# Keys turned later, vector work dealt out anew and a new layout of activations in a two-block transformer kernel

## What is computed

```
h  = modulate(rms_norm(x), shift, scale);  hc = the same for ctx
q, k, v = split(h @ w_qkv); q = rms_norm(q) * q_g; k = rms_norm(k) * k_g   # per head; k, v also of hc
s  = [q k^T / sqrt(128) + bias, masked;  q kc^T / sqrt(128)];  o = softmax(s) [v; vc]
x  = x + gate_msa * (o @ w_o)
x  = x + gate_ffn * (silu(conv3(h2 @ w_gate)) * conv3(h2 @ w_up)) @ w_down
```

## Time and profile before

| | |
|---|---|
| median of 3 runs | 2519.28 us (2518.7 to 2519.54) |
| the profiled execution | 2518.32 us, span 2516.6 us |
| PE busy | 2468.2 us, 98% of the span, 13260 matmuls |
| DVE, ACT, POOL busy | 71%, 46%, 9% |
| chain that ended last | PE 88%, DVE 5%, DMA 4%, issue 2%, ACT 1% |
| DMA | 519.06 MB, mean 206 GB/s |

### The profile page before, as it was taken

How to read it: one execution, slowest core, us unless ns; L and a number is a source line. 1 busy time by engine, 2 the same in 40 slices (tenths; PEclk the granted TensorE clock), 3 DMA queues, 4 the chain that set the end, 5 groups by cost and what they waited for, 6 DMA issues and landing times.

```text
span 2516.6 us, 38054 instructions
## 1 busy us (share of the span) xinstructions
PE 2468.2 (98%) x13260; PEld 2119.8 (84%) x13260; DVE 1786.5 (71%) x2395; ACT 1161.1 (46%) x1512; POOL 218.1 (9%) x251
## 2 busy tenths in 40 slices
PE   9999999999999999998999999989999999999999
PEld 8989988888888888887887888877888888888887
DVE  6667757898888877876666776776667656665666
ACT  4455545534535445553223333334555535553453
POOL 5000000000000000312111011130200000000000
PEclk9999999999999999999999999999999999999999
DMA  8655577887787778756556565665655665656665
GB/s 268 183 135 154 165 252 243 278 292 238 262 274 240 263 241 277 242 166 182 171 178 191 186 186 180 197 202 156 191 188 183 194 194 175 193 191 194 182 187 173
DMA packets 281385, 519.06 MB, mean 206 GB/s; under 512 B 33822, under 2 KB 105256, under 8 KB 280512
## 3 DMA queue, kind: packets, MB, share of 16 engines
q1 hardware_dynamic: 255968, 403.67, 51.0%
q0 software_dynamic: 25120, 113.89, 14.4%
q10 hardware_dynamic: 192, 0.05, 0.0%
HBM read 515.35 MB, written 6.90 MB: 208 GB/s over the span
## 4 chain that ended last, share of the span: by engine, by line
PE 88%; DVE 5%; DMA 4%; issue 2%; ACT 1%; POOL 0%; DVEq 0%; SPq 0%; POOLq 0%; ACTq 0%
PE ps L2029 33%; PE ps L2058 22%; PE ps L2061 11%; PE ps L2435 11%; PE ps L2021 3%; DMA arena<-in_w_ada 2%; DVE arena L1572 2%; PE ps L2513 1%; PE ps L2494 1%; DVE wlo L1240 1%; PE ps L2446 1%; DMA raw<-in_na_w_qkv 1%; DMA raw<-in_w_in 1%; PE ps L2503 1%; PE ps L2350 0%
## 5 line engine op out<-in xcount | busy, mean ns | idle before, releaser
L1240 DVE TENSOR_TENSOR wlo<-raw,whi 128x1024 fp32r<-128x1024 f32 (+1 forms) x776 | 930.4, 1210 | 411.8 <-ACT whi L727 390.2
L727 ACT ACTIVATE whi<-raw 128x1024 fp32r<-128x1024 f32 (+1 forms) x776 | 797.0, 1036 | 840.4 <-PE ps L2029 372.2
L2029 PE MATMUL ps<-whi,act 128*128 128x512 f32 (+3 forms) x2736 | 823.8, 382 | 11.3 <-POOL act L694 5.7
L2058 PE MATMUL ps<-act,whi 128*128 128x512 f32 x2400 | 657.6, 395 | 1.4 <-DVE act L1903 1.3
L2029 PEld LDWEIGHTS ps<-whi,act 128*128 128x128 f32 x2736 | 505.0, 188 | 104.5 <-POOL act L694 5.7
L2029 PE MATMUL ps<-wlo,act 128*128 128x512 f32 (+3 forms) x1368 | 520.0, 380 | 0.0
L2058 PEld LDWEIGHTS ps<-act,whi 128*128 128x128 f32 x2400 | 410.1, 189 | 56.6 <-DVE act L1903 1.6
L2061 PEld LDWEIGHTS ps<-act,wlo 128*128 128x128 f32 x2400 | 369.5, 189 | 51.7
L2061 PE MATMUL ps<-act,wlo 128*128 128x256 f32 x2400 | 383.9, 281 | 0.0
L2435 PE MATMUL ps<-whi,act 128*128 128x512 f32 x1024 | 325.0, 399 | 1.6 <-issue 1.6
L1572 DVE SCALAR_TENSOR_TENSOR arena<-arena,cond 128x768 f32<-128x768 f32 (+1 forms) x330 | 291.2, 905 | 19.4 <-DMA arena<-in_w_ada 16.0
(11 more groups left out here) (317 smaller groups left out, 1776.9 us busy)
## 6 DMA issues: line engine op xcount, KB each, us to landing
arena<-in_w_ada POOLq DMA_DIRECT2D x128, 768.0 KB, 6.1
raw<-in_ffn_w_up SPq DMA_DIRECT2D x160, 512.0 KB, 4.3
raw<-in_w_mlp_in SPq DMA_DIRECT2D x128, 512.0 KB, 4.8
raw<-in_w_mlp_out SPq DMA_DIRECT2D x128, 512.0 KB, 4.9
raw<-in_ffn_w_down SPq DMA_DIRECT2D x84, 512.0 KB, 4.4
raw<-in_na_w_qkv SPq DMA_DIRECT2D x128, 256.0 KB, 3.3
raw<-in_w_in SPq DMA_DIRECT2D x64, 384.0 KB, 4.0
raw<-in_w_in SPq DMA_DIRECT2D x32, 512.0 KB, 4.0
```

Of the source, the lines that this page charges most:

```text
L727: act.activation(a, b, ACT.Copy).then_inc(hi_done, 1)
L1240: dve.tensor_tensor(a, b, c, ALU.subtract).then_inc(lo_done, 1)
L2029: ins = pe.matmul(o, a, b, start=start and i == 0, stop=last and i == 2, skip_group_check=True)
L2058: pe.matmul(Z[q][:, c, :].rearrange("p (h t) -> p h t", h=2), kn(whi, j)[:, kk, P * c:P * c + P], act2[:, :, k, 0:S], start=k == 0, stop=k ...
```

## The change

The activations are laid out as [chunk][set][high or low][256], so that the merged matmul reads 512 values in one run; every reader and writer of them follows. Keys are turned behind unit 0 of the next turn, just ahead of the queries, and not behind unit 10; ScalarE's copy of them moves with it, ahead of the queries' copy. VectorE's key sums are done in two steps, m = 8 and 9, the inverse norms at 10, the scaling at 11. The second sum of the condition's products is turned into bank X[0] and not X[2], with its waits moved. The context tiles' keys go to banks 0 and 1, own rows' to 2 and 3, so that the first units wait only for the first half of PSUM. The terms are dealt out anew. The gate row's write moves behind the loads of the last turn, its read into the output projection, ahead of chunk 8; POOL's second load stands before the third chunk. ScalarE makes the high parts of the heads four at a time and earlier.

```diff
-FIRST_TERMS = {3: range(16, 19), 4: range(19, 22), 5: range(22, 25), 6: range(25, 28), 7: range(28, 32)}
-TURN_TERMS = [range(0, 3), range(3, 6), range(6, 9), range(9, 12), range(12, 15), range(15, 19), range(19, 23), range(23, 28),
-              range(28, 29), range(29, 30), range(30, 31), range(31, 32)]
+FIRST_TERMS = {4: range(16, 19), 5: range(19, 22), 6: range(22, 25), 7: range(25, 28), 8: range(28, 29), 9: range(29, 30),
+               10: range(30, 31), 11: range(31, 32)}
+TURN_TERMS = [range(0, 3), range(3, 6), range(6, 9), range(9, 12), range(12, 15), range(15, 19), range(19, 23), range(23, 27),
+              range(27, 29), range(29, 30), range(30, 31), range(31, 32)]
+LAST_TERMS = {6: range(0, 3), 7: range(3, 6), 8: range(6, 8), 13: range(8, 10), 14: range(10, 12), 15: range(12, 14), 16: range(14, 16)}
...
-        act2 = sb("act2", [P, 2, KC, 2 * S], F32R)
-        ahi, alo = act2[:, 0], act2[:, 1]
-        both = act2.rearrange("p h k t -> p h (k t)")
+        act2 = sb("act2", [P, KC, 2, 2, S], F32R)
+
+        def ahi(k, t0, n):
+            return act2[:, k, t0 // S, 0, t0 % S:t0 % S + n]
...
         def ctx_rows(h, c, t0, n):
-            at = (512 * c + 512) % (512 * KC)
-            return both[:, h, at + t0:at + t0 + n]
+            return act2[:, (c + 1) % KC, 0, h, t0:t0 + n]
...
             attention_loads(0, range(4, 8))
-            gate_row_out(0, 32)
             with pool.Fori(1, 8) as i:
                 attention_loads(i)
-            gate_rows_in(0, gb)
+            gate_row_out(0, 32)
             attention_loads(8, range(1))
             for c in range(14):
-                if c == 4:
+                if c == 2:
                     attention_loads(8, range(1, 2))
+                if c == 8:
+                    gate_rows_in(0, gb)
                 pool.wait_ge(a_hi, OT_AT + c + 1)
...
+            def key_out(i):
+
+                act.wait_ge(k_turn, i)
+                act.activation(kT, ps[:, 5:7, :], ACT.Copy, scale=cols[:, R_KG:R_KG + 1]).then_inc(k_out, 1)
...
                     if m == 1 and not first:
+                        key_out(i)
                         query_out(i)
...
-                            act.activation(kv[:, r, :], ps[:, r, :], ACT.Copy).then_inc(k_row, 1)
-                    if m == 9:
+                            act.activation(kv[:, r, :], ps[:, (r + 2) % 4, :], ACT.Copy).then_inc(k_row, 1)
+                    if m == 10:
                         inv_rms(16, k_rms, i * 2 + 1, 8)
-                    if m == 11:
-                        act.wait_ge(k_turn, i + 1)
-                        act.activation(kT, ps[:, 5:7, :], ACT.Copy, scale=cols[:, R_KG:R_KG + 1]).then_inc(k_out, 1)
...
             act.wait_ge(unit_used, U_WO - 3)
             heads_hi(range(4))
+            act.wait_ge(unit_used, U_WO - 2)
+            heads_hi(range(4, 8))
             query_rows(8, U_WO)
             split(U_WO, 3)
             for m in range(9):
                 if m >= 2:
                     attend_a(8, m - 2, 1)
                 split(U_WO, 4 + m)
-                if m < 5:
-                    heads_hi((2 * m + 4, 2 * m + 5))
+                if m == 0:
+                    heads_hi(range(8, 12))
                 if m == 1:
+                    key_out(8)
                     query_out(8)
+                    heads_hi((12, 13))
...
-                    if m == 8:
-                        key_sums(i)
-                    if m == 9:
+                    if m in (8, 9):
+                        key_sums(i, ((0, 1), (2, 3))[m - 8])
+                    if m == 11:
                         key_norm(i)
...
                 split(U_WO, 4 + m)
+                ada_terms(8, LAST_TERMS.get(m, ()))
...
             def ffn_gate(j):
 
-                if 13 <= j < 19:
-                    ada_terms(8, ((0, 1, 2), (3, 4, 5), (6, 7, 8), (9, 10, 11), (12, 13), (14, 15))[j - 13])
+                ada_terms(8, LAST_TERMS.get(j, ()))
...
-                        pe.matmul(Z[q][:, c, :].rearrange("p (h t) -> p h t", h=2), kn(whi, j)[:, kk, P * c:P * c + P],
-                                  act2[:, :, k, 0:S], start=k == 0, stop=k == KC - 1, skip_group_check=True)
+                        pe.matmul(Z[q][:, c, :], kn(whi, j)[:, kk, P * c:P * c + P],
+                                  act2[:, k, 0].rearrange("p h t -> p (h t)"), start=k == 0, stop=k == KC - 1, skip_group_check=True)
...
             def first_keys():
 
-                for q in range(2):
-                    pe.wait_ge(drained[q], D_MLP[q])
+                pe.wait_ge(drained[0], D_MLP[0])
                 pe.wait_ge(a_lo, TURN_AT[4])
...
+                pe.wait_ge(drained[1], D_MLP[1])
                 for m in range(4):
...
             def second_slot(i):
-                ada_turn(acc2, X[2], [(ada_done, i * 8 + (64 - 4)), (k_out, i)])
+                ada_turn(acc2, X[0], [(ada_done, i * 8 + (64 - 4)), (q_row, i)])
...
                     if m == 0:
+                        turn_keys(i)
                         turn_queries(i)
                         second_slot(i)
...
-                    if m == 10:
-                        turn_keys(i, first)
```

More of the change, by code:

```diff
@@ L629, in turn @@
                     k = slice(2 * at, 2 * at + 2)
-                    pool.tensor_tensor(alo[:, k, off:off + S], turned_f[:, at % 2],
-                                       ahi[:, k, off:off + S].bitcast(F32), ALU.subtract).then_inc(a_lo, 2)
+                    pool.tensor_tensor(alo(k, off, S), turned_f[:, at % 2],
+                                       ahi(k, off, S).bitcast(F32), ALU.subtract).then_inc(a_lo, 2)
             def turn_lo(e, at):
@@ L736, in turn @@
                         b = shift(k) if shift else 0.0
-                        act.activation(ahi[:, k, off:off + S], z, ACT.Identity, scale=gain(k), bias=b).then_inc(a_hi, 1)
+                        act.activation(ahi(k, off, S), z, ACT.Identity, scale=gain(k), bias=b).then_inc(a_hi, 1)
             pieces = [slice(512 * c, 512 * c + 512) for c in range(4)]
@@ L1253, in turn @@
                         z = X[at % 4][:, c * S:c * S + S]
-                        hi = f(ahi[:, k, off:off + S])
+                        hi = f(ahi(k, off, S))
                         if shift:
@@ L1258, in turn @@
                         else:
-                            dve.scalar_tensor_tensor(out=alo[:, k, off:off + S], in0=z, scalar=gain(k), in1=hi,
+                            dve.scalar_tensor_tensor(out=alo(k, off, S), in0=z, scalar=gain(k), in1=hi,
                                                      op0=ALU.mult, op1=ALU.subtract).then_inc(a_lo, 1)
@@ L1776, in query_norm, with key_sums @@
                 rows_scaled(qr, 32, 4, q_norm)
-            def key_sums(i):
-                for r in range(4):
+            def key_sums(i, tiles):
+                for r in tiles:
                     dve.wait_ge(k_row, i * 4 + (r + 1))
                     row_sums(kv[:, r, 0:S], 16, r)
-                own.wait()
-                dve.sem_inc(k_rms, 1)
+                if tiles[-1] == 3:
+                    own.wait()
+                    dve.sem_inc(k_rms, 1)
             def key_norm(i):
@@ L2019, in columns @@
                 wh, wl = kn(whi, j)[:, kk, c0:c0 + n], kn(wlo, j)[:, kk, c0:c0 + n]
-                for i, (a, b) in enumerate(terms(wh, wl, ahi[:, k, t0:t0 + tn], alo[:, k, t0:t0 + tn], True)):
+                for i, (a, b) in enumerate(terms(wh, wl, ahi(k, t0, tn), alo(k, t0, tn), True)):
                     ins = pe.matmul(o, a, b, start=start and i == 0, stop=last and i == 2, skip_group_check=True)
@@ L2027, in rows @@
                 wh, wl = kn(whi, j)[:, kk, c0:c0 + n], kn(wlo, j)[:, kk, c0:c0 + n]
-                for i, (a, b) in enumerate(terms(wh, wl, ahi[:, k, t0:t0 + P], alo[:, k, t0:t0 + P], False)):
+                for i, (a, b) in enumerate(terms(wh, wl, ahi(k, t0, P), alo(k, t0, P), False)):
                     ins = pe.matmul(o, a, b, start=start and i == 0, stop=last and i == 2, skip_group_check=True)
@@ L2434, in key_value_unit @@
                         for y, (a, b) in enumerate(terms(wh, wl, tile_rows(r, 0, k), tile_rows(r, 1, k), False)):
-                            ins = pe.matmul(ps[:, r, :], a, b, start=k == 0 and y == 0, stop=k == KC - 1 and y == 2,
+                            ins = pe.matmul(ps[:, (r + 2) % 4, :], a, b, start=k == 0 and y == 0, stop=k == KC - 1 and y == 2,
                                             skip_group_check=True)
@@ L2473, in turn_queries, with turn_keys @@
                 ins.then_inc(q_turn, 1)
-            def turn_keys(i, first):
-                pe.wait_ge(k_norm, i + 1)
-                if not first:
-                    pe.wait_ge(n_t, i * 4 + AHEAD)
-                    pe.wait_ge(n_pt, i * 4 + AHEAD)
+            def turn_keys(i):
+                pe.wait_ge(k_norm, i)
+                pe.wait_ge(n_t, i * 4 + (AHEAD - 4))
+                pe.wait_ge(n_pt, i * 4 + (AHEAD - 4))
                 for h in range(2):
```

36 lines of the change are left out of this document (19 added, 17 removed).

## The result

The changed kernel takes **2491.24 us**, median of four runs (2490.77 to 2493.81), against 2519.41 for the kernel before in the same session (2518.7 to 2520.74). The ratio is 0.989, interval 0.9873 to 0.9907: 28 us faster. The profiled execution is 2491.34 us with a span of 2489.7. Against the profiled execution of before (2518.32) that is 27.0 us; 34 were forecast. 2484 was too low by 7, and 2491 lies within the range of 2468 to 2498.

What follows compares the result with a forecast made beforehand. The prediction took TensorE (busy 98% of the span) as the bound, with its waits and the clock drops behind them; 15.3 + 6.6 + 3.3 + 9.5 - 1 = 33.7, or 34 us off 2518.3 gave 2484, range 2468 to 2498.

Steps and rivals of the forecast that it cites:

- Layout 0: Merged matmul of the up projections: reading one run of 512 instead of two of 256 gains 0, at most 12 us.
- rival F: Halves side by side slow TensorE's reads by 5 ns on 12,000 matmuls: slower, 2544 us; chance 0.03.
- First key units 1.5: First key units: starting with context tiles in long-drained banks gains 1.5 of a 1.6 us wait; ends 0 and 1.6.
- First turn 15.3: First turn: without the gate row's write, queries start 12.5 us earlier, first key units included, plus 2.8 of clock; ends 8 and 15.3.
- rival E: The gate write is innocent and the first turn's weight blocks come late anyway: 12 us less gained, 2496; chance 0.03.
- What the write does to DMA: First turn: the write holds DMA to 31 GB/s; a skill rule, read as excluding this, would cost the sum 12 us.
- Six middle turns 6.6: Middle turns: the 2.5 us key wait goes, a new 1.4 us query wait comes; 1.1 gained each; ends 0 and 15.
- only the 0.49 us that it then waited for ScalarE's split goes: Middle turns: VectorE's work up to the last term stays the same; only its 0.49 us wait for ScalarE's split disappears.
- Clock 3.3: Middle turns: two clock drops behind 2.5 us waits go, 3.4 and 3.3 us halved, gaining 3.3; ends 0 and 3.3.
- Last turn into the output projection 9.5 - 1: Unit 16 starts about 7.5 us earlier, plus half of 3.9; 9.5, ends 4 and 12; minus 1 for a clock drop.
- a gap of about 3 between units 0 and 1: Output projection: a new gap of some 3 us between its first two units, which may drop the clock once.
- Rival D: The gate write's new place in the output projection delays weight blocks: up to 10 us lost, 2494; chance 0.08.

Runs made afterwards that it cites:

- experiment 1: The kernel before with only the new layout of the activations: 2520.18 us, ratio 1.0003.
- experiment 3: The kernel before with only the gate row moved: written after POOL's loop over turns, read at chunk 8 of the output projection; 2516.29 us, ratio 0.9982.
- experiment 2: The changed kernel with the gate row's write back in its old place, ahead of POOL's loop over turns: 2497.45 us, ratio 0.9915.
- experiment 6: The changed kernel with VectorE's loop over head turns 1 to 7 written out as seven turns: 2482.46 us, ratio 0.9847.
- experiment 5: The changed kernel with the gate row's write in the middle of turn 7's w_ada loads: 2489.08 us, ratio 0.9876.
- experiment 4: The changed kernel with VectorE's query norm ahead of its split at m = 0 in turns 1 to 7: 2484.07 us, ratio 0.9861.
- experiment 8: The changed kernel with the edits of experiment 4 and experiment 5, and POOL's second load of the last turn back at the fifth chunk: 2480.71 us, ratio 0.984.
- experiment 9: Experiment 8 with the gate row written in four pieces, in turns 1 to 4, those turns of POOL's loop written out: 2478.99 us, ratio 0.9834.
- experiment 10: Experiment 9 with VectorE's loop over head turns written out as in experiment 6: 2472.23 us, ratio 0.9814.

## Why the prediction was right or wrong, point by point

- **Layout 0**: right, shown by experiment 1. The same run answers rival F. F asks how one engine's own reads lie side by side, which a rule on waiting for other engines doesn't settle; 2520.18 against 2518.49 us does.
- **First key units 1.5**: right, 1.5. The first key unit starts 0.9 earlier (1114.53 against 1115.41) though the MLP ends 0.9 later, and the transposes between the key units give 0.3 back. Only the two profiles show it.
- **First turn 15.3**: right, 15.4 by the starts of the queries' units. That the write holds up the first turn is shown from both sides, with 8.3 (experiment 3) and 9.8 (experiment 2); rival E is out. The other 5.6 to 7 came with the rest: the 1.5 of the first key units, and the keys' turn, whose wait of 3.4 stays when the write alone moves and is gone in the change. The prediction laid some 12 us at the write's door (rival E), so its sum is right and its cause only in part.
- **What the write does to DMA.** Behind it 31 and 37 GB/s were measured at its old place, 18 at the new one and 34 behind a quarter of it. The prediction read the Trainium skill's rule that a DMA engine takes its rings in turn, packet by packet (DMA: Bandwidth & Descriptors, section on queues, rings and completion order), as one by which the write can't hold back SP's loads. That reading is out. The rule itself is not tested: it says whose packet is next and not how long one takes. In the troughs the DMA engines are listed as busy for 0.46, 0.33, 0.38 and 0.98 of the time, so three of the four are not full; what holds the loads inside DMA stays open.
- **Six middle turns 6.6**: the term that failed, 2.8 measured. The mechanism was right (no wait at the keys, a new one at the queries, set by VectorE) and the sign of the parts too, but the new wait is 2.05 and not 1.4. The step that failed is "only the 0.49 us that it then waited for ScalarE's split goes". It didn't go, since it was the loop's turn (experiment 6). Against unit 8's start the queries were scaled at 20.29 before (1333.18 - 1312.89) and 20.27 after (1318.22 - 1297.95), where the prediction had them 0.49 earlier. The line starts 0.35 later after the change (1.77 against 1.42), but that is only how long its first term is listed, 1.91 before and 1.56 after (the earlier trace rows have it merged with three more):

```profile
1314.31 1.91 DVE L1572 SCALAR_TENSOR_TENSOR arena<-arena,cond 128x384 f32<-128x384 f32 x1 [1.79 <-DMA arena<-in_w_ada]
```

  It ends 3.33 after unit 8's start in both, and from there to the end of the scaling it takes 16.96 and 16.94. So 0.47 of the 0.66 that the new wait is longer are this step; 0.14, from the end of the scaling to TensorE's start, were left out of the sum, and 0.05 TensorE is there sooner.
- **Clock 3.3**: 1.4 measured; one drop stayed, and the two of before had cost 1.5 each, by the lengths of their turns (70.4 against 68.9). It followed from the same step: of six waits of 2.05 us none dropped it in experiment 2, one in the change and two in experiment 5; waits of 0.9 didn't in any of the profiles that had them (experiments 4, 6, 8, 9).
- **Last turn into the output projection 9.5 - 1**: the sum was right with 8.2, its parts less so, and that is luck in part. Up to unit 16 it was 6.0, where 7.5 less the 1 for the clock had been forecast; behind unit 16 it was 2.2, for 2. I had put a gap of about 3 between units 0 and 1. It was 4.8, ahead of unit 0, with 6.9 us at half clock. The chain, in the timelines of DVE, ACT and POOL of the changed kernel:

```profile
1649.48 0.62 DVE L1585 SCALAR_TENSOR_TENSOR arena<-arena,cond 128x384 f32<-128x384 f32 x1 [2.12 <-DMA arena<-in_w_ada]
```

```profile
1652.38 0.21 ACT L1069 ACTIVATE nst<-nst 128x8 f32<-128x8 f32 x1 [5.05 <-DVEq L1798]
...
1653.73 2.55 ACT L1116 ACTIVATE act<-arena 128x256 fp32r<-128x256 f32 x8
```

```profile
1642.83 1.19 POOL L681 DMA_DIRECT2D gate_row_scratch<-mods  x1
...
1654.21 2.37 POOL L700 TENSOR_TENSOR act<-arena,act 128x256 fp32r<-128x256 f32 x2 [5.78 <-ACT act L1116]
```

  The write is issued at 1642.83, in the order of POOL's work where the prediction had it: in the old place of the read the earlier trace rows, but 18.7 us earlier, like all work there. The prediction gave it the old time, near 1661.5, and looked for the trough near 1665; it lies from 1647 to 1653. It delays the `w_ada` transfer that VectorE needs; VectorE then sums the keys late, ScalarE waits 5.05 us for the sums with the copies of the heads behind it, and POOL with it. I had looked for weight blocks and not for the transfer that VectorE's line hangs on. Against that the drain's wait shrank to 0.9, where I had 1 to 1.5, and the waits for POOL behind unit 1 are gone; these two are read from the two profiles, no run takes them out.
- **Rival D** (up to 10 lost at the write's new place): the place does cost, by another road than the one it named: 1.6 us up to unit 16 in experiment 2, 3.1 in experiment 5 and 3.6 in experiment 3, what the clock loses there included.

## What to carry to other kernels

When a wait is moved off the path, the next one is set by an engine's whole line of work since its last outside event; add that line up from the rows, gaps included, and ask of each gap whether its releaser was really late. A loop on an engine that isn't the bottleneck is not free once that engine's line ends last: here it cost 1.1 us a turn. A transfer of single elements like this one (it took 9 to 15 us to land) should stand where nobody needs a load for as long, and the search for who needs one has to include the small loads that other engines' lines hang on.

## What was not expected of the hardware

- On VectorE the loop's turn shows as 0.48 us, each split behind a term starts 0.08 later inside the loop than outside (0.12 against 0.04), and the reduction 0.20 (0.24 against 0.04). How much of it is fetching and how much the counting of waits and addresses was not separated.
- A write of 512 single elements takes hardly less time to land than one of 2048: 10.7 to 12.0 us for the four pieces, 9.2 to 15.0 for the whole ones in the runs above. The whole ones spread so widely that the two can't be told apart by it; the length of the trough is the better measure.
- The spread between runs goes with the clock. Of the 39 runs of the kernel before in the three sessions, the 25 with a mean granted clock of 0.994 average 2520.5 us, the nine with 0.995 average 2517.6. The kernel before, with 2.5 us waits, ranged over 7.3, 5.3 and 7.3 us in its three sessions of 13 runs; in the profile of experiment 1, where the same waits stand, there are three drops in the middle turns, and in that of before two. The versions of experiments 9 and 10, whose waits there are 0.9 us or none, range over 1.0 us each (four runs); those of experiments 4, 6 and 8, with the same waits of 0.9, over 1.7 to 2.4, and the change, with 2.05, over 3.0. So the 3.3 us that the prediction took for two drops were one throw of several. What decides whether a wait of 2 to 2.5 us drops the clock stays open.
